# RWKV's token shift by three SBUF transfers in place of fp32 matmuls with a shift table, in a two-block transformer kernel

## The reference

```python
def _rwkv7_branch(cols, mu, w0, w2, a0, a2, g2, k_k, k_a, r_k, gn_gain):
    B, S, _ = cols.shape
    prev = jnp.pad(cols[:, :-1], ((0, 0), (1, 0), (0, 0)))
    cols = cols + (prev - cols) * mu
    r, k, v, xw, xa, xg = jnp.split(cols, [...], axis=-1)
    w_pre = -jax.nn.softplus(-(w0 + jnp.tanh(xw) @ w2)) - 0.5
    ...
```

## Time and profile before

| | |
|---|---|
| times | 1355.03 us (median of 3 runs, 1353.13 to 1361.8) |
| profiled execution | 1358.5 us, span 1356.7 us |
| mean granted TensorE clock | 0.956 of full speed |
| TensorE matmul busy | 1263.4 us, 93% |
| VectorE busy | 754.3 us, 56% |
| ScalarE busy | 496.6 us, 37% |
| chain that ended last | PE 85%, DVE 5%, ACT 4%, issue 3% |

### The profile page before, as it was taken

How to read it: one execution, slowest core, us unless ns; L and a number is a source line. 1 busy time by engine, 2 the same in 40 slices (tenths; PEclk the granted TensorE clock), 3 DMA queues, 4 the chain that set the end, 5 groups by cost and what they waited for, 6 DMA issues and landing times.

```text
span 1356.7 us, 19736 instructions
## 1 busy us (share of the span) xinstructions
PE 1263.4 (93%) x8384; PEld 1149.7 (85%) x8384; DVE 754.3 (56%) x940; ACT 496.6 (37%) x690; POOL 63.8 (5%) x69
## 2 busy tenths in 40 slices
PE   4999999999999999998999999999997989979896
PEld 3789889888999998798989889999995777757775
DVE  4586537354655564774654545555565545555453
ACT  3354313113333334464212024333343553335532
POOL 1002001000000000020010000000002000030000
PEclk9999999999999999998989899999998998989988
DMA  7542212424444444432212434444427233272220
GB/s 285 209 149 91 94 63 94 156 95 184 187 186 186 186 185 151 151 125 94 76 51 105 173 131 180 186 186 186 185 100 185 95 108 139 96 189 93 98 90 31
DMA packets 35731, 188.26 MB, mean 139 GB/s; under 512 B 12113, under 2 KB 13009, under 8 KB 14033
## 3 DMA queue, kind: packets, MB, share of 16 engines
q1 hardware_dynamic: 34080, 175.89, 35.9%
q10 hardware_dynamic: 1440, 8.55, 1.6%
q0 software_dynamic: 144, 2.89, 0.5%
HBM read 182.07 MB, written 5.24 MB: 138 GB/s over the span
## 4 chain that ended last, share of the span: by engine, by line
PE 85%; DVE 5%; ACT 4%; issue 3%; DVEq 1%; DMA 1%; POOLq 0%; POOL 0%; SPq 0%; ACTq 0%
PE bank L993 18%; PE bank L636 16%; PE bank L661 9%; PE bank L1009 9%; PE bank L972 4%; PE bank L956 4%; PE bank L1128 3%; PE bank L775 2%; PE bank L747 2%; PE bank L624 2%; DVE in_low L1552 2%; PE bank L763 2%; ACT in_high L1228 1%; PE bank L876 1%; PE bank L884 1%
## 5 line engine op out<-in xcount | busy, mean ns | idle before, releaser
L1552 DVE TENSOR_TENSOR in_low<-ring,in_high 128x2048 fp32r<-128x2048 f32 x72 | 165.7, 2305 | 79.1 <-ACT in_high L1228 79.1
L636 PE MATMUL bank<-in_high,h_high 128*128 128x512 f32 x352 | 150.9, 429 | 30.3 <-DVE in_low L1552 30.3
L1228 ACT ACTIVATE in_high<-ring 128x2048 fp32r<-128x2048 f32 x72 | 137.2, 1909 | 109.3 <-PE bank L636 99.7
L636 PE MATMUL bank<-in_low,h_high 128*128 128x512 f32 x352 | 144.8, 411 | 0.0
L636 PE MATMUL bank<-in_high,x_low 128*128 128x512 f32 x352 | 144.2, 410 | 0.0
L993 PE MATMUL bank<-h_high,gate_split 128*128 128x256 f32 x704 | 130.7, 283 | 4.1 <-DVE gate_split L1919 3.9
L993 PE MATMUL bank<-h_high,up_split 128*128 128x256 f32 x704 | 128.4, 281 | 0.0
L661 PE MATMUL bank<-h_high,in_high 128*128 128x256 f32 x384 | 118.4, 308 | 0.5 <-DVE in_low L1552 0.5
L1009 PE MATMUL bank<-act_split,down_split 128*128 128x256 f32 x960 | 118.2, 283 | 0.0
L1009 PEld LDWEIGHTS bank<-act_split,down_split 128*128 128x128 f32 x960 | 116.4, 192 | 0.0
L993 PEld LDWEIGHTS bank<-h_high,gate_split 128*128 128x128 f32 x704 | 111.6, 191 | 5.6 <-DVE gate_split L1919 4.8
(11 more groups left out here) (309 smaller groups left out, 2361.0 us busy)
## 6 DMA issues: line engine op xcount, KB each, us to landing
ring<-w_in_dram SPq DMA_DIRECT2D x72, 1024.0 KB, 4.9
ring<-w_gate_up_dram SPq DMA_DIRECT2D x44, 1024.0 KB, 8.0
ring<-w_down_dram SPq DMA_DIRECT2D x22, 1024.0 KB, 4.8
ring<-w_out_dram SPq DMA_DIRECT2D x16, 1024.0 KB, 6.2
ring<-p_all_dram SPq DMA_DIRECT2D x6, 1024.0 KB, 4.9
x_kept<-scratch ACTq DMA_DIRECT2D x4, 1024.0 KB, 4.2
x<-x_kept ACTq DMA_DIRECT2D x4, 1024.0 KB, 7.5
table<-tables_dram POOLq DMA_DIRECT2D x1, 2818.0 KB, 12.6
```

The costliest lines, as they stand in the source:

```text
L636: last = mm(bank[(n - n % 2 + t) % 4][:], a, b, start=c == 0 and i == 0, stop=c == KT - 1 and i == 2)
L1228: f(in_high[n % 2][:], ring[:, n % 4, :].rearrange("p (k n) -> p k n", k=KT), ACT.Copy).then_inc(done.sem, 1)
L1552: tt(in_low[n % 4][:], ring[:, n % 4, :].rearrange("p (k n) -> p k n", k=KT), in_high[n % 2][:].bitcast(F32), ALU.subtract).then_inc(low.s ...
```

## The change

The tables `dshift` and `carry` and the function `rw_difference` go away. `previous` is a view of scratch columns 0 to 2047 as (p, t, 1024 columns). VectorE sets its row (0, 0) to zero, after waiting for the readers of `fresh`. SyncE, ahead of the load of weight tile 7, waits for that zero and for `g_out` 4, and issues three transfers from `rw` to `previous`, one partition down: rows 16 to 127 (112 of them, both tiles in one), rows 1 to 15, and row 127 of tile 0 to row 0 of tile 1. VectorE then computes `(previous - rw) * mu + rw` in three operations of 128x2048, with a drain between each two.

```diff
-    t["dshift"] = (j == i[None] - 1) * 1.0 - (j == i[None])
-    t["carry"] = (j == P - 1) * (i[None] == 0) * 1.0
...
-        rs_d = sig("rw_diff", 4)
+        rs_z = sig("rw_first_row", 1)
+        rs_d = sig("rw_previous_in", 3, 16)
...
+        previous = carve(0, 2048)[0].rearrange("p (t c) -> p t c", t=NT)
...
                 for n in range(len(IN_STARTS)):
+                    if n == 7:
+
+                        sp.wait_ge(*g_out.after(l, 4))
+                        sp.wait_ge(*rs_z.after(l, 1))
+                        for a, b in ((16, P), (1, 16)):
+                            sp.dma_start(previous[a:b], rw[a - 1:b - 1]).then_inc(rs_d.sem, 16)
+                        sp.dma_start(previous[0:1, 1], rw[P - 1:P, 0]).then_inc(rs_d.sem, 16)
                     free = [g_full.after(l, n - 3)] if n >= 4 else [ffn_before(l, n)] if l else []
...
-            def rw_difference(l):
...
-                rw_difference(l)
                 group(l, 5)
...
                 spread(2 * l)
+                dve.wait_ge(*f_full.after(l, 1))
+                dve.wait_ge(*x_saved.after(l, 1))
+                nc.vector.memset(previous[0:1, 0], 0.0).then_inc(rs_z.sem, 1)
                 in_split(l, 4, in_hi, in_lo)
...
                 in_split(l, 6, in_hi, in_lo)
-                dve.wait_ge(*x_saved.after(l, 1))
                 dve.wait_ge(*mu_in.after(l, 1))
-                tmp = [lo, w_ex, w_t1, w_t2]
-                for i in range(4):
-                    dve.wait_ge(*rs_d.after(l, i + 1))
-                    tt(tmp[i], bank[4 + i][:], w_mu[:, (i % 2) * 512:(i % 2 + 1) * 512], ALU.mult)
-                fence()
-                for i in range(4):
-                    c = rw[:, i // 2, (i % 2) * 512:(i % 2 + 1) * 512]
-                    last = tt(c, c, tmp[i], ALU.add)
+                dve.wait_ge(*rs_d.after(l, 3))
+                tt(previous, previous, rw, ALU.subtract)
+                fence()
+                tt(previous, previous, put(w_mu, 1, NT), ALU.mult)
+                fence()
+                last = tt(rw, rw, previous, ALU.add)
                 last.then_inc(rs_u.sem, 1)
```

More of the change, by code:

```diff
@@ L788, in attention @@
                     values(h)
-            def rw_difference(l):
-                pe.wait_ge(*g_out.after(l, 4))
-                pe.wait_ge(consts_in.sem, 16)
-                pe.wait_ge(*norms.spread_out.after(2 * l, 1))
-                pe.wait_ge(*f_out.after(l, 1))
-                for t in range(NT):
-                    for half in range(2):
-                        o, c = bank[4 + 2 * t + half][:], slice(half * 512, half * 512 + 512)
-                        last = mm(o, tab["dshift"], rw[:, t, c], start=True, stop=t == 0)
-                        if t == 1:
-                            last = mm(o, tab["carry"], rw[:, 0, c], start=False, stop=True)
-                        last.then_inc(rs_d.sem, 1)
             def rw_lora_transposes(l):
```

## The result

The changed kernel takes 1360.03 us (median of 22 runs, 1356.36 to 1365.74) against 1353.76 us for the kernel before on the same chip (median of 22, 1350.61 to 1362.12): ratio 1.004, 95% interval 1.0027 to 1.0053. So it is slower by about 5.4 us by the ratio (3.7 to 7.2; the medians differ by 6.3): no gain, within 1%, and inside the forecast's range. The time is 2.5 us above the forecast's 1357.5; the loss, 5.4 us, is about twice the 2.5 that were forecast. (The kernel before also measured 1.3 us faster here than the median that the forecast started from.)

What follows compares the result with a forecast made beforehand. TensorE, busy 93% of the span, was taken to bound the kernel. Per layer -5.15 + 4.79 (waits before group 7) + 1.6 (clock) = +1.24 us; two layers +2.5 on 1355.03 gave 1357.5 us, range 1351.5 to 1363.5.

Steps and rivals of the forecast that it cites:

- Matmuls removed, up to group 6: TensorE, groups 4 to 6: without the shift matmuls group 5 starts at 54.82, not 59.97, gaining 5.15 us per layer.
- Memset: VectorE before split 4: zeroing one row of 1024 columns takes 0.9 us, hidden in a 1.08 us wait for ScalarE.
- The transfers: SyncE's three shift transfers: issue from 52.48, 4.9 us plus 0.6 for issues, landing about 58.0, hidden until 59.01.
- SyncE's wait: Weight tile 7's load, behind the three issues: issued about 54.1, landed about 61.6, hidden with 5 us to spare.
- VectorE's shift: Three 128x2048 operations from 59.01: 7.03 us with drains instead of 5.08, so 1.95 us longer per layer.
- Where the gain goes: TensorE waits 3.1 us before the transposes and again before group 7, which starts about 71.2; 0.36 of 5.15 us left.
- The clock: TensorE's pause before group 7 lowers its clock: 1.6 us lost per layer, bounds 0 and 2.6.
- the group at 36.25: Group of 24 matmuls at half clock after a weak stretch: 7.22 us against 5.48, 1.74 lost; model for the clock price.
- the forecast's starting point: Median time of the kernel before that the forecast added its change to: 1355.03 us.
- The clock staying up: Rival: group 7 runs at full speed despite the pause; -0.7 us, 1354.3 us; chance 0.15.
- The gain in full: Rival: VectorE does not hold the shift and all matmul time is gained; -10.3 us, 1344.7 us; chance 0.02.
- Late transfers: Rival: transfers paid one after another land at 62.0, 3.0 us late per layer; +8.5 us, 1363.5 us; chance 0.17.

Runs made afterwards that it cites:

- keep_matmuls: Changed kernel with six matmuls of 512 columns per layer, results unused, put back between groups 4 and 5; 1354.19 us against 1355.35 before, 0.9982.
- two_operations: Changed kernel without the multiplication by `mu`, so two VectorE operations of 128x2048 instead of three; 0.9937 of the kernel before.
- fill_pause: Changed kernel with useless matmuls in TensorE's pause, four calls ahead of the LoRA transposes and two ahead of group 7; 0.9994 of the kernel before.
- no_transfers: Changed kernel without its three transfers per layer, so the shift computes on stale rows; 0.9971 of the kernel before.
- split7_ahead: Changed kernel with VectorE's split 7 right behind the shift and ScalarE's group 5 ahead of its three activations; 1350.28 us against 1353.53 before, 0.9975.
- reordered: Changed kernel with orders rewritten: `own` before split 6, last 256 columns first, split 7 and other work moved forward; 1339.83 us against 1354.44 before, 0.9889.
- small_first: Changed kernel with the three transfers issued smallest first (1, 15, 112 rows), tile 7's load still behind them; 1361.67 us, one time.
- after_again: The changed kernel itself, unaltered, measured again beside its variants; 1360.61 us against 1354.44 for the kernel before, 1.0042.

## Why the forecast was right, and what it missed

**Matmuls removed, up to group 6.** Right: groups 4 to 6 run without a gap, group 6 ends at 69.73 - 4.16 = 65.57 us (forecast 65.75), and the whole 5.15 us is there. keep_matmuls shows the same from the other side.

**Memset.** 0.9 forecast, 0.91 measured. Split 4 behind it started at 45.49, against 45.46 before, with the whole stretch 0.12 us earlier.

**The transfers.** A term that was mis-sized. I took 4.9 us plus 0.6 for three issues, 5.5 in all, landing at 58.0 and hidden until 59.01. The last of the three landed 7.31 us after the first issue, at 59.70, and VectorE waited 0.83 us (0.56 in the second layer). Both parts were short: SyncE needed 0.63 + 1.01 us before the third issue, and the last landing came 5.67 after that. By the Trainium skill's "DMA: Bandwidth & Descriptors" ("Rules for kernel authors", two transfers serialize) and its fixed cost, which it gives for transfers issued by GpSimd, the estimate was 60.9. The measurement lies between: transfers do queue, as the packets of the 4 KB row show, but less was paid than three fixed costs in a row.

**SyncE's wait.** Right in effect, wrong in size: tile 7 was issued at 56.17 and not 54.1, the third issue alone taking 2.09 us, and was still hidden. (The 2.6 us of the forecast for data behind the shift's has no row.)

**VectorE's shift.** 7.03 forecast, 64.53 + 2.29 - 59.80 = 7.02 measured. The five small operations end at 69.30 + 0.28 = 69.58, 2.73 us behind ScalarE's first activation (66.85), as forecast.

**Where the gain goes.** Right: TensorE waits 4.16 us before the transposes, released by L1695, and 0.66 before group 7 (forecast 3.1 and 1.7). The sums agree, 4.8 and 4.82, but only because the transposes between, at the low clock, took 71.85 - 0.66 - 69.73 = 1.46 us instead of 0.66; `rl_s` itself came late. From the first matmul of group 4, group 7 was to start at 71.2 - 49.21 = 21.99 us in the chain's terms; it started at 22.76 and 22.49. The 0.77 and 0.50 are the late landing (VectorE waited 0.83 and 0.56). The forecast's small gain of 0.36 us per layer turned into a small loss.

**The clock.** Right in kind (0.50 from 68 on, back at 78), too cheap, the other mis-sized term: 1.6 us per layer forecast, 8.55 - 5.48 = 3.07 and 7.17 - 5.48 = 1.69 measured; 2.75 and 2.82 in the second measurement. I had put it near the 1.74 of the group at 36.25; three of the four lie above my bound of 2.6. By two_operations 0.30 of each is the start after a wait and not the clock; without it they are 2.77, 1.39, 2.45 and 2.52, and one lies above.

The misses add up: 2.5 forecast, 0.77 + 0.50 for the landing, 1.47 + 0.09 for the clock, makes 5.3; the two stretches lost 5.34. These are parts of the same stretches, so the sum has to agree and proves nothing by itself; what separates the parts are keep_matmuls, fill_pause and no_transfers. That the time came within 2.5 us of the forecast is partly luck: both terms were too small, and the forecast's starting point was 1.3 us high.

**The rivals.** The clock staying up would have given -0.7 us; fill_pause, with useless matmuls to keep it up, measured 0.9994, which is -0.8 us, though its stretches are 1.2 us above before. The gain in full did not come. Late transfers came true by 0.8 us, not 3.0.

**Open.** Why the clock outside the two stretches is withheld less in no_transfers (52 us), split7_ahead (52) and reordered (51) than in the kernel before (56 to 57) and in the changed kernel (56 to 59). The column and the windows show that it is; which places fall was looked at in one profile each, and no run isolated what decides it. The 5.6 us of reordered's gain that are clock are therefore measured, but not explained. The same holds for keep_matmuls' last tenths.

## What to carry to other kernels

Work taken off the engine that bounds is worth only what the next wait behind it allows: follow the order of the other engines to the next operand, and rewrite that order with the change, or nothing is gained (1.004 without, 0.989 with). Here pauses of 3.7 to 5.9 us in all took TensorE's clock down (the kernels in the table whose group 7 took over 7 us), and that made a loss (1.004) of a change that is neutral with the clock kept up (0.9994); a change of this kind should be judged after its pause is closed. Count a transfer's issue on its queue as well as its flight, and choose the rows of an SBUF copy so that they divide over the DMA engines (112 and 15 rows here; 127 in one cost 73 us more, in one run).

## What the hardware showed that I had not expected

- A pause of 1.7 + 1.3 us with six small matmuls between, in both layers of two_operations, left the clock up; pauses of 3.2 + 0.7 us (no_transfers) and of 3.7 (split7_ahead) took it down. The pause of 1.93 us that ends at 121.10 in the kernel before was followed by a fall as well, and the same pause in reordered was not, so the length alone does not decide.
- An issue on SyncE isn't a constant: 0.59, 0.96 and 2.09 us for three transfers in a row of 112, 15 and 1 rows. The single row takes 0.59 us when it is issued first (small_first), 2.09 behind the other two, and 16.56 behind the one of 127 rows.
- A copy from SBUF to SBUF one partition down, 896 KB, lands 6.0 us after its issue as the last of three (small_first), against 4.9 for 1 MB from HBM.
- The clock withheld over a whole execution came to 50.9 to 65.7 us between kernels that differ in a few instructions around group 5, and the stretches themselves hold at most 8.5 of these. It is also most of the scatter between runs: over the 23 runs of the kernel before beside after_again, spans differ by 14.6 us and span x clock has a standard deviation of 1.2.
